# LayerNorm of a convolution module on one core: the variance of the first 256 tokens from the mean of seven channel blocks, corrected by the eighth

## The chip, the cores and the metric

The kernel runs on one core of one Trainium2 chip. The metric is the device time in microseconds (us) of one execution, as the median over runs. Five engines work at once, each through its own queue of instructions in order: TensorE (PE in the profile), VectorE (DVE), ScalarE (ACT), GpSimd (POOL) and the sync engine (SP), which only issues transfers. They wait for one another through semaphores. SBUF is the on-chip memory, PSUM the memory into which PE accumulates.

## The reference

Two layers with 512 tokens of 1024 channels. Layer 0 has a convolution module as its mixer, layer 1 an attention; each is followed by a squared-ReLU MLP. Only this part of layer 0 is touched:

```python
def layernorm(x, g, b):
    xf = x.astype(jnp.float32)
    mu = jnp.mean(xf, axis=-1, keepdims=True)
    var = jnp.mean(jnp.square(xf - mu), axis=-1, keepdims=True)
    y = (xf - mu) * lax.rsqrt(var + LN_EPS)
    return (y * g.astype(jnp.float32) + b.astype(jnp.float32)).astype(x.dtype)

def conformer_conv(h, pw1_w, pw1_b, dw_w, dw_b, ln_g, ln_b, pw2_w, pw2_b):
    a = h @ pw1_w + pw1_b
    u, gate = jnp.split(a, 2, axis=-1)
    u = u * jax.nn.sigmoid(gate)
    y = lax.conv_general_dilated(u, dw_w[:, None, :], ...) + dw_b   # 31 taps, causal, one filter per channel
    y = layernorm(y, ln_g, ln_b)
    y = jax.nn.silu(y)
    return y @ pw2_w + pw2_b
```

The mean and the variance are taken over the 1024 channels, for each token by itself.

## The kernel before, in words

Activations lie with channels on the 128 partitions: `y[:, k, :]` is channel block k (k = 0 to 7, `KB` = 8) for all 512 tokens. A sum over channels therefore needs PE: a matmul with a matrix of ones. Float32 matmuls are issued by PE as two passes each, so the profile counts two MATMUL rows for one in the code. `EARLY` is tokens 0 to 255, `LATE` tokens 256 to 511; the norm handles EARLY first, so that the second pointwise product (`second_conv`) can begin on it.

The order of work is written out by hand, engine by engine.

- **The last taps.** The taps of the depthwise convolution are shared by PE (`conv`, L1055 on), DVE (`tap`), ACT and POOL (`tap_sums`, L672). Block 7 is the last: DVE joins its partial sums (L2342), waits for POOL's sums (L2345), waits for PE's taps and writes `y[:, 7, :]` (L2348). In the meantime PE has begun the channel sum of blocks 0 to 6 into the PSUM bank STAT (L1079, L1080).
- **The mean.** PE adds block 7 to that sum (L1121). DVE then subtracts sum/D from each block (`conv_sub`, L2352): eight EARLY blocks, then three LATE ones.
- **The variance, EARLY.** ACT squares each EARLY block (L1707) into `m`. PE sums the squares over channels with eight calls of `token_columns` (L948), each two matmuls that move one column of ones. ACT takes the root (L1712), DVE the reciprocal (L2212), PE spreads it over the partitions (L955).
- **The norm loop, DVE.** For k = 0 to 8: `conv_norm` (L2362) multiplies `y` by the spread reciprocal in PSUM; one or no LATE `conv_sub`; `conv_rest` (L2368) makes the low part of the split of the result, `hlo = tmp - hhi`, after ACT's SiLU and copy (L1722, L1725); `late_add` (L2376) adds up LATE squares, which POOL makes (L803). So 5 LATE subtractions lie before the loop and 3 in it.
- **PE beside the loop.** `second_conv` multiplies each EARLY block by four weight units, 12 matmuls of 256 columns a block (L894 to L896), as soon as `hlo` of that block is there. After block 5 it waits for the seventh `late_add` (semaphore `c_add`), sums the LATE squares (L948), and after block 6 it spreads the LATE reciprocal (L955). The rest of the module, the MLP and layer 1 follow in series.
- **POOL's own queue** here: `tap_sums` of block 7, then four `conv_lo` (L677, 1024 elements per partition each, the low parts of the weights of the second pointwise product), then the eight LATE squares (L803).

`keep_warm` (L905) issues small matmuls with no use for their result. What matters of an operand is where it lies: `conv_sub` and `conv_norm` read one tensor of SBUF and one of PSUM; `conv_rest` and `late_add` read two tensors of SBUF.

```python
            for k in range(KB + 1):
                if k < KB:
                    conv_norm(0, k)
                if k < 3:
                    conv_sub(1, 5 + k)
                if k >= 1:
                    conv_rest(0, k - 1)
                if k >= 2:
                    late_add(k - 1)
```

Of the kernel before, what the change touches and what calls it, by code (L numbers as in the profile page):

```python
# [10 lines left out]
P = 128  # L11
# [197 lines left out]
def build(nc, x, g_mix_pre, g_mix_post, g_ffn_pre, g_ffn_post, conv_pw1_w, conv_pw1_b, conv_dw_w,  # L209
# [168 lines left out]
    form_hi, form_nth, form_lo, lo_nth = s["glu_s"], KB, s["c_ready"], 2 * KB  # L378
    h_made, made_nth = s["c_sub"], 2 * KB
    x_copy = nc.dram_tensor("x_copy", (P, KB * S), F32, kind="Internal").ap()  # L380
# [114 lines left out]
    with nc.Block() as block:  # L495
# [128 lines left out]
        def _(pool):  # L624
# [176 lines left out]
            for k in range(KB):  # L801
                pool.wait_ge(s["c_sub"], KB + k + 1)
                g.tensor_tensor(m[:, k, LATE], y[:, k, LATE], y[:, k, LATE], ALU.mult).then_inc(s["c_late"], 1)  # L803
# [74 lines left out]
        def _(pe):  # L878
# [180 lines left out]
            def conv(j, r, more=0):  # L1059
# [17 lines left out]
                if more:  # L1077
                    pe.wait_ge(s["y_sum"], y_sums(KB - 1) + 1)
                    pe.matmul(psum[:, STAT, :], ones[:, :], sumsq[:, :], start=True, stop=False)  # L1079
                    pe.matmul(psum[:, STAT, :], ones[:, :], y[:, KB - 2, :], start=False, stop=False)  # L1080
                    pe.wait_ge(s["diag"], KB - 1)
# [36 lines left out]

            keep_warm(WARM_TAPS)
            pe.wait_ge(s["y_done"], KB)  # L1120
            pe.matmul(psum[:, STAT, :], ones[:, :], y[:, KB - 1, :], start=False,  # L1121
                      stop=True).then_inc(s["mean"], 1)
            keep_warm(WARM_SUB, 0)
            for k in range(KB):
                pe.wait_ge(s["c_sq"], k + 1)
                mm = token_columns(OUTP, 0, m[:, k, :], (0, 1), k == 0, k == KB - 1)
            mm.then_inc(s["c_sum"], 1)
            keep_warm(WARM_ROOT, 0)
            pe.wait_ge(s["irms_done"], NTH[ST_VAR[0]])
# [14 lines left out]
            for kb in range(KB):  # L1144
                second_conv(0, (kb,), range(4))
                if kb == 5:
                    pe.wait_ge(s["c_add"], KB - 1)
# [327 lines left out]
        def _(act):  # L1475
# [229 lines left out]
            for k in range(KB):  # L1705
                act.wait_ge(s["c_sub"], k + 1)
                a.activation(m[:, k, EARLY], y[:, k, EARLY], ACT.Square).then_inc(s["c_sq"], 1)  # L1707

            def conv_root(h):
                tiles = (slice(0, 2), slice(2, 4))[h]  # L1710
                act.wait_ge(s["c_sum"], h + 1)
                a.activation(rms[:, tiles], psum[:, (OUTP, STAT)[h], tiles], ACT.Sqrt, scale=1.0 / D,  # L1712
                             bias=eps[:, 1:2]).then_inc(s["root"], 1)

# [457 lines left out]
        def _(dve):  # L2172
# [166 lines left out]
            for i in range(DVE_TAPS - MORE_TAPS):  # L2339
                tap(KB - 1, 1, i, DVE_TAPS - MORE_TAPS)  # L2340
            dve.wait_ge(s["tap"], DVE_TAPS * KB - MORE_TAPS)
            d.tensor_tensor(psum[:, 0, :], psum[:, 0, :], acc1[:, 1, :], ALU.add).then_inc(s["acc"], 1)  # L2342
            dve.wait_ge(s["acc"], KB)
            dve.wait_ge(s["y_sum"], y_sums(KB - 1) + (POOL_SUMS + 1))
            d.tensor_tensor(acc1[:, 1, :], psum[:, 0, :], y[:, KB - 1, :], ALU.add).then_inc(s["acc"], 1)  # L2345
            dve.wait_ge(s["acc"], KB + 1)
            dve.wait_ge(s["conv_done"], KB)
            d.tensor_tensor(y[:, KB - 1, :], psum[:, 5, :], acc1[:, 1, :], ALU.add).then_inc(s["y_done"], 1)  # L2348

            def conv_sub(h, k):  # L2350
                rows = (EARLY, LATE)[h]
                d.scalar_tensor_tensor(y[:, k, rows], psum[:, STAT, rows], -1.0 / D, y[:, k, rows], ALU.mult,  # L2352
                                       ALU.add).then_inc(s["c_sub"], 1)

            def conv_norm(h, k):
                rows = (EARLY, LATE)[h]
                if k == 0:
                    dve.wait_ge(s["bcast"], NTH[ST_VAR[h]])
                dve.wait_ge(s["c_sub"], KB * h + k + 1)
                if h:  # L2360
# [10 lines left out]
            def late_add(k):  # L2371

                dve.wait_ge(s["c_late"], k + 1)
                if k > 1:
                    dve.wait_ge(s["c_add"], k - 1)
                d.tensor_tensor(sumsq[:, LATE], m[:, 0, LATE] if k == 1 else sumsq[:, LATE], m[:, k, LATE],  # L2376
                                ALU.add).then_inc(s["c_add"], 1)

            dve.wait_ge(s["mean"], 1)
            for k in range(KB):  # L2380
                conv_sub(0, k)
            for k in range(3):
# [746 lines left out]
```

## Time and profile before

| what | value |
|---|---|
| median of 3 runs | 1138.76 us (1137.33 to 1139.12) |
| the profiled execution, its own time | 1139.56 us |
| its span, first to last instruction | 1137.8 us |
| mean granted TensorE clock in it | 0.996 of full |
| PE, DVE, ACT, POOL busy, share of the span | 98%, 82%, 67%, 26% |

The time axis of all rows is the span of the profiled execution. Its own time lies 1.76 us above the span and 0.80 us above the median. The norm of the convolution lies at about 150 to 186 us of that axis. A busy share is an average over the whole span; what limits a stage is read from the rows of that stage. In the timeline views a row is one or several alike instructions in order of time: start, length, engine, line of the kernel, operation, what it writes and reads, count, and in brackets how long the engine idled before it and who released it.

### The profile page before, as it was taken

The numbers are of one execution on the slowest core, as the hardware profiler recorded it, in microseconds if no ns is written. First come the engines' busy times: TensorE is split into PE (matmuls) and PEld (weight loads), VectorE is DVE, ScalarE is ACT, GpSimd is POOL, SyncE is SP. The second block draws the span as 40 slices with busy tenths as digits, with TensorE's granted clock in tenths as the row PEclk, the third lists the DMA queues.
The fourth block names the chain that finished last, engine by engine and source line by source line (L and its number), as shares of the span: only waits on it lengthen the run. The fifth ranks groups of instructions, "written<-read, shape, count | busy, mean of one in ns | idle before, by whom it ended". The sixth has DMA issues, their size and how long they took to land. (4 is left out here: it accounts for less than half of the span.)

```text
span 1137.8 us, 18248 instructions
## 1 busy us (share of the span) xinstructions
PE 1116.8 (98%) x6462; PEld 978.5 (86%) x6462; DVE 934.6 (82%) x1348; ACT 765.5 (67%) x1266; POOL 291.7 (26%) x269
## 2 busy tenths in 40 slices
PE   9999999999999999999999999999999999999997
PEld 7788888978898998998887888878888998998986
DVE  6899965679889689688798888894789889688788
ACT  6778868556685484675787777776566783674764
POOL 5688870221211020112421111100312020111014
PEclk9999989999999999999999999999999999999999
DMA  5322141275866676595222423232476776567673
GB/s 162 105 74 74 37 124 42 61 221 149 180 174 132 200 156 158 134 237 112 57 56 67 104 65 87 84 84 74 140 205 156 184 167 180 120 145 193 159 197 99
DMA packets 137268, 146.73 MB, mean 129 GB/s; under 512 B 5949, under 2 KB 108349, under 8 KB 136682
## 3 DMA queue, kind: packets, MB, share of 16 engines
q1 hardware_dynamic: 112300, 109.68, 30.7%
q0 software_dynamic: 24816, 35.92, 19.8%
q8 instruction: 45, 0.74, 0.3%
q14 instruction: 29, 0.24, 0.1%
q10 hardware_dynamic: 78, 0.16, 0.0%
HBM read 137.09 MB, written 6.29 MB: 126 GB/s over the span
## 5 line engine op out<-in xcount | busy, mean ns | idle before, releaser
L1525 ACT ACTIVATE whi<-mraw 128x1024 fp32r<-128x1024 f32 x212 | 221.4, 1055 | 150.3 <-PE psum L1219 92.0
L2190 DVE TENSOR_TENSOR wlo<-mraw,whi 128x1024 fp32r<-128x1024 f32 x212 | 256.7, 1222 | 71.5 <-ACT whi L1525 71.1
L1217 PE MATMUL psum<-whi,aop_hi 128*128 128x512 f32 x448 | 176.1, 393 | 1.0 <-ACT acc L1815 0.7
L1218 PE MATMUL psum<-wlo,aop_hi 128*128 128x512 f32 x448 | 174.5, 390 | 0.0
L1219 PE MATMUL psum<-whi,aop_lo 128*128 128x512 f32 x448 | 174.5, 389 | 0.0
L887 PE MATMUL psum<-hhi,whi 128*128 128x512 f32 x376 | 150.8, 401 | 0.8 <-DVE wlo L2179 0.5
L889 PE MATMUL psum<-hhi,wlo 128*128 128x512 f32 x376 | 147.0, 391 | 0.0
L888 PE MATMUL psum<-hlo,whi 128*128 128x512 f32 x376 | 146.8, 390 | 0.0
L1204 PE MATMUL psum<-xlo,whi 128*128 128x256 f32 x384 | 108.7, 283 | 0.0
L1205 PE MATMUL psum<-hhi,wlo 128*128 128x256 f32 x384 | 108.7, 283 | 0.0
L1203 PE MATMUL psum<-hhi,whi 128*128 128x256 f32 x384 | 108.6, 283 | 0.0
L1217 PEld LDWEIGHTS psum<-whi,aop_hi 128*128 128x128 f32 x448 | 84.1, 188 | 21.7 <-DVE acc L2653 2.5
L1219 PEld LDWEIGHTS psum<-whi,aop_lo 128*128 128x128 f32 x448 | 84.1, 188 | 17.8
L1218 PEld LDWEIGHTS psum<-wlo,aop_hi 128*128 128x128 f32 x448 | 84.2, 188 | 16.8
L889 PEld LDWEIGHTS psum<-hhi,wlo 128*128 128x128 f32 x376 | 70.6, 188 | 15.5
L887 PEld LDWEIGHTS psum<-hhi,whi 128*128 128x128 f32 x376 | 70.7, 188 | 14.7 <-issue 1.8
L888 PEld LDWEIGHTS psum<-hlo,whi 128*128 128x128 f32 x376 | 70.8, 188 | 12.9
L1203 PE MATMUL psum<-hlo,whi 128*128 128x256 f32 x288 | 81.6, 283 | 0.2 <-DVE pair L2594 0.2
L1205 PE MATMUL psum<-hlo,wlo 128*128 128x256 f32 x288 | 81.5, 283 | 0.0
L2269 DVE SCALAR_TENSOR_TENSOR psum<-upad,vec,psum 128x512 f32<-128x512 f32 x116 | 78.0, 749 | 3.4 <-ACT psum L1657 3.4
L761 POOL DMA_DIRECT2D mraw<-in_mlp_w_down x24 | 28.9, 1203 | 182.3 <-DVE wlo L2190 182.3
L1204 PEld LDWEIGHTS psum<-xlo,whi 128*128 128x128 f32 x384 | 73.7, 192 | 0.2
(314 smaller groups left out, 2834.8 us busy)
## 6 DMA issues: line engine op xcount, KB each, us to landing
mraw<-in_mlp_w_up SPq DMA_DIRECT2D x64, 512.0 KB, 7.0
mraw<-in_mlp_w_down SPq DMA_DIRECT2D x64, 512.0 KB, 5.5
mraw<-in_mlp_w_down POOLq DMA_DIRECT2D x40, 512.0 KB, 7.2
mraw<-in_mlp_w_up POOLq DMA_DIRECT2D x24, 512.0 KB, 7.1
wraw<-in_conv_pw_w SPq DMA_DIRECT2D x20, 512.0 KB, 4.5
wraw<-in_attn_w_in SPq DMA_DIRECT2D x16, 512.0 KB, 5.0
x_copy<-xT SPq DMA_DIRECT2D x2, 2048.0 KB, 7.4
xT<-x_copy SPq DMA_DIRECT2D x2, 2048.0 KB, 11.4
```

Of the source, the lines that this page charges most:

```text
L887: pe.matmul(o, whi[:, u, kb, :], xhi, start=start, stop=False)
L888: pe.matmul(o, whi[:, u, kb, :], xlo, start=False, stop=False)
L889: return pe.matmul(o, wlo[:, u, kb, :], xhi, start=False, stop=stop)
L1203: pe.matmul(o, wh[:, w], xh[:, k, :], start=first, stop=False, skip_group_check=True)
L1204: pe.matmul(o, wh[:, w], xl[:, k, :], start=False, stop=False, skip_group_check=True)
L1205: mm = pe.matmul(o, wl[:, w], xh[:, k, :], start=False, stop=k == 3, skip_group_check=True)
L1217: pe.matmul(o, ah, wh, start=kt == 0 and (not kept or c == 0), stop=False)
L1218: pe.matmul(o, ah, wl, start=False, stop=False)
L1219: return pe.matmul(o, al, wh, start=False, stop=kt == 3 and (not kept or c == CHUNKS - 1))
L1525: a.activation(split_unit(whi, e), raw_unit(l, c, e_), ACT.Copy).then_inc(s["m_hi"], 1)
L2190: d.tensor_tensor(split_unit(wlo, e), raw_unit(l, c, e_), split_unit(whi, e).bitcast(F32), ALU.subtract).then_inc(s["m_ready"], 1)
L2269: d.scalar_tensor_tensor(dst, upad[:, r, t:t + S], vcol(V_DW + t, j), src, ALU.mult, ALU.add).then_inc(s["tap"], 1)
```

## The change

For the EARLY tokens only, the variance is taken in another way. Blocks 0 to 6 are complete before block 7, so their sum S7 stands in PSUM while the last taps still run. DVE subtracts S7/(D-128) from blocks 0 to 6 (`first_sub`), and from the partial sum `acc1` of block 7, so that block 7 when finished has had the same number taken off. ACT squares these. What is left of the mean is the channel sum of block 7 alone over D, since the other seven now sum to zero; the sum of squares about the true mean is the sum of the squares less (sum of block 7)^2/D. DVE makes that correction on two columns (`tot`), and ACT's root reads it. The remaining mean is subtracted from EARLY by eight `conv_sub` that run beside the sums.

To sum fewer columns, DVE adds squares in pairs, blocks 0+1, 2+3, 4+5 (`early_add`, two SBUF tensors), so PE does five `token_columns` of squares and one of block 7 in place of eight. All eight LATE subtractions now lie in the norm loop. Two of the groups of `keep_warm` (2 and 3 matmuls) are gone, and the sum for the mean of LATE (with its own last step) comes after the column sums.

```diff
                     pe.matmul(psum[:, STAT, :], ones[:, :], sumsq[:, :], start=True, stop=False)
-                    pe.matmul(psum[:, STAT, :], ones[:, :], y[:, KB - 2, :], start=False, stop=False)
+                    pe.matmul(psum[:, STAT, :], ones[:, :], y[:, KB - 2, :], start=False,
+                              stop=True).then_inc(s["mean"], 1)
...
-            keep_warm(WARM_TAPS)
+            for k in (0, 2):
+                pe.wait_ge(s["c_add"], k // 2 + 1)
+                token_columns(OUTP, 0, m[:, k, :], (0, 1), k == 0, False)
             pe.wait_ge(s["y_done"], KB)
-            pe.matmul(psum[:, STAT, :], ones[:, :], y[:, KB - 1, :], start=False,
+            pe.matmul(psum[:, 1, LATE], ones[:, :], y[:, KB - 1, EARLY], start=True,
                       stop=True).then_inc(s["mean"], 1)
-            keep_warm(WARM_SUB, 0)
-            for k in range(KB):
+            token_columns(5, 0, y[:, KB - 1, :], (0, 1), True, True).then_inc(s["mean"], 1)
+            pe.wait_ge(s["c_add"], 3)
+            token_columns(OUTP, 0, m[:, 4, :], (0, 1), False, False)
+            for k in (KB - 2, KB - 1):
                 pe.wait_ge(s["c_sq"], k + 1)
-                mm = token_columns(OUTP, 0, m[:, k, :], (0, 1), k == 0, k == KB - 1)
+                mm = token_columns(OUTP, 0, m[:, k, :], (0, 1), False, k == KB - 1)
             mm.then_inc(s["c_sum"], 1)
+            pe.matmul(psum[:, STAT, LATE], ones[:, :], y[:, KB - 1, LATE], start=False, stop=True,
+                      skip_group_check=True).then_inc(s["mean"], 1)
             keep_warm(WARM_ROOT, 0)
...
+            def first_sub(t, sem):
+
+                d.scalar_tensor_tensor(t, psum[:, STAT, EARLY], -1.0 / (D - P), t, ALU.mult,
+                                       ALU.add).then_inc(sem, 1)
+
+            def early_add(k):
+
+                dve.wait_ge(s["c_sq"], k + 2)
+                d.tensor_tensor(m[:, k, EARLY], m[:, k, EARLY], m[:, k + 1, EARLY],
+                                ALU.add).then_inc(s["c_add"], 1)
...
+            dve.wait_ge(s["mean"], 1)
+            for k in range(KB - 1):
+                first_sub(y[:, k, EARLY], s["c_sub"])
             dve.wait_ge(s["acc"], KB)
             dve.wait_ge(s["y_sum"], y_sums(KB - 1) + (POOL_SUMS + 1))
             d.tensor_tensor(acc1[:, 1, :], psum[:, 0, :], y[:, KB - 1, :], ALU.add).then_inc(s["acc"], 1)
             dve.wait_ge(s["acc"], KB + 1)
+            first_sub(acc1[:, 1, EARLY], s["acc"])
+            early_add(0)
+            early_add(2)
+            dve.wait_ge(s["acc"], KB + 2)
             dve.wait_ge(s["conv_done"], KB)
             d.tensor_tensor(y[:, KB - 1, :], psum[:, 5, :], acc1[:, 1, :], ALU.add).then_inc(s["y_done"], 1)
...
-            dve.wait_ge(s["mean"], 1)
-            for k in range(KB):
+            early_add(4)
+            dve.wait_ge(s["mean"], 2)
+            conv_sub(0, 0)
+            conv_sub(0, 1)
+            dve.wait_ge(s["mean"], 3)
+            d.tensor_copy(tot[:, 0:2], psum[:, 5, 0:2]).then_inc(s["x_tot"], 1)
+            conv_sub(0, 2)
+            dve.wait_ge(s["x_tot"], 2)
+            d.scalar_tensor_tensor(tot[:, 2:4], tot[:, 0:2], -1.0 / D, psum[:, 5, 0:2], ALU.mult,
+                                   ALU.mult).then_inc(s["x_tot"], 1)
+            for k in range(3, 5):
                 conv_sub(0, k)
-            for k in range(3):
-                conv_sub(1, k)
+            dve.wait_ge(s["c_sum"], 1)
+            dve.wait_ge(s["x_tot"], 3)
+            d.tensor_tensor(tot[:, 2:4], psum[:, OUTP, 0:2], tot[:, 2:4], ALU.add).then_inc(s["x_tot"], 1)
+            conv_sub(0, 5)
+            conv_sub(0, 6)
             inverse(ST_VAR[0], slice(0, 2))
-            for k in range(3, 5):
-                conv_sub(1, k)
+            conv_sub(0, 7)
+            dve.wait_ge(s["mean"], 4)
             for k in range(KB + 1):
                 if k < KB:
                     conv_norm(0, k)
-                if k < 3:
-                    conv_sub(1, 5 + k)
+                if k < KB:
+                    conv_sub(1, k)
```

Semaphore counts elsewhere follow, and ACT's root of EARLY reads `tot` where it read PSUM. Three places show the order of instructions.

**DVE, from the last join of block 7 to the first subtractions.** Names: `acc_77` is `acc1`; 128x256 is one block of EARLY or LATE. Before:

```order
L2342 TENSOR_TENSOR psum<-psum,acc_77 128x512
L2345 TENSOR_TENSOR acc_77<-psum,y 128x512
L2348 TENSOR_TENSOR y<-psum,acc_77 128x512
L2352 SCALAR_TENSOR_TENSOR y<-psum,y 128x256 x11
L2212 RECIPROCAL irms<-rms 128x2
L2352 SCALAR_TENSOR_TENSOR y<-psum,y 128x256 x2
```

and in the changed kernel:

```order
L2365 TENSOR_TENSOR psum<-psum,acc_77 128x512
L2356 SCALAR_TENSOR_TENSOR y<-psum,y 128x256 x7
L2371 TENSOR_TENSOR acc_77<-psum,y 128x512
L2356 SCALAR_TENSOR_TENSOR acc_77<-psum,acc_77 128x256
L2362 TENSOR_TENSOR m<-m 128x256 x2
L2378 TENSOR_TENSOR y<-psum,acc_77 128x512
L2362 TENSOR_TENSOR m<-m 128x256
L2384 SCALAR_TENSOR_TENSOR y<-psum,y 128x256 x2
L2416 COPY tot<-psum 128x2
L2384 SCALAR_TENSOR_TENSOR y<-psum,y 128x256
L2419 SCALAR_TENSOR_TENSOR tot<-tot,psum 128x2
L2384 SCALAR_TENSOR_TENSOR y<-psum,y 128x256 x2
```

Seven subtractions now stand ahead of the wait for POOL's sums, and two of the pairwise additions (L2362) ahead of the instruction that finishes block 7 (L2378).

**DVE in the norm loop, k = 2 and 3.** Before:

```order
L2362 TENSOR_TENSOR y<-y,psum 128x256
L2352 SCALAR_TENSOR_TENSOR y<-psum,y 128x256
L2368 TENSOR_TENSOR hlo<-tmp,hhi 128x256
L2376 TENSOR_TENSOR sumsq<-m 128x256
L2362 TENSOR_TENSOR y<-y,psum 128x256
L2368 TENSOR_TENSOR hlo<-tmp,hhi 128x256
L2376 TENSOR_TENSOR sumsq<-sumsq,m 128x256
```

and in the changed kernel:

```order
L2394 TENSOR_TENSOR y<-y,psum 128x256
L2384 SCALAR_TENSOR_TENSOR y<-psum,y 128x256
L2400 TENSOR_TENSOR hlo<-tmp,hhi 128x256
L2408 TENSOR_TENSOR sumsq<-m 128x256
L2394 TENSOR_TENSOR y<-y,psum 128x256
L2384 SCALAR_TENSOR_TENSOR y<-psum,y 128x256
L2400 TENSOR_TENSOR hlo<-tmp,hhi 128x256
L2408 TENSOR_TENSOR sumsq<-sumsq,m 128x256
```

From k = 3 on each turn has a subtraction (L2384) that it did not have.

**PE between the last tap and the spread.** Before:

```order
L1073 MATMUL psum<-uhi,diaglo 128x512
L905 MATMUL psum<-ones 128x128 x2
L1121 MATMUL psum<-y,ones 128x512
L905 MATMUL psum<-ones 128x128 x3
L948 MATMUL psum<-ones,m 128x1 x16
L905 MATMUL psum<-ones 128x128
L955 MATMUL psum<-ident,irms 128x128 x2
```

and in the changed kernel:

```order
L1073 MATMUL psum<-uhi,diaglo 128x512
L948 MATMUL psum<-ones,m 128x1 x4
L1124 MATMUL psum<-y,ones 128x256
L948 MATMUL psum<-ones,y 128x1 x2
L948 MATMUL psum<-ones,m 128x1 x6
L1133 MATMUL psum<-y,ones 128x256
L905 MATMUL psum<-ones 128x128
L955 MATMUL psum<-ident,irms 128x128 x2
```

Four of the ten column sums of squares now stand ahead of block 7's own sum, six behind it.

## Rows read from the trace of the kernel before

**Rows 1.** The page, busy time of each engine over the span

```profile
PE 1116.8 (98%) x6462; PEld 978.5 (86%) x6462; DVE 934.6 (82%) x1348; ACT 765.5 (67%) x1266; POOL 291.7 (26%) x269
```

**Rows 2.** Timeline of PE, 151 to 175 us

```profile
151.44 0.61 PE L905 MATMUL psum<-ones 128*128 128x128 f32 x4
152.46 1.13 PE L1121 MATMUL psum<-y,ones 128*128 128x512 f32 x2 [0.41 <-DVE y L2348]
...
154.54 5.24 PE L948 MATMUL psum<-ones,m 128*128 128x1 f32 x32 [0.29 <-ACT m L1707]
...
160.34 1.22 PE L955 MATMUL psum<-ident,irms 128*128 128x128 f32 x4
...
164.13 0.36 PE L894 MATMUL psum<-hhi,whi 128*128 128x256 f32 x1
...
172.83 0.50 PE L948 MATMUL psum<-ones,sumsq 128*128 128x1 f32 x4
...
174.71 0.60 PE L955 MATMUL psum<-ident,irms 128*128 128x128 f32 x4
```

**Rows 3.** Timeline of DVE, 149 to 162 us

```profile
149.85 0.69 DVE L2345 TENSOR_TENSOR acc<-psum,y 128x512 f32<-128x512 f32 x1 [2.99 <-POOL y L672]
151.71 0.69 DVE L2348 TENSOR_TENSOR y<-psum,acc 128x512 f32<-128x512 f32 x1 [1.17 <-PE psum L1073]
153.62 3.73 DVE L2352 SCALAR_TENSOR_TENSOR y<-psum,y 128x256 f32<-128x256 f32 x11 [1.22 <-PE psum L1121]
160.11 0.17 DVE L2212 RECIPROCAL irms<-rms 128x2 f32<-128x2 f32 x1 [2.76 <-ACT rms L1712]
...
161.59 0.42 DVE L2362 TENSOR_TENSOR y<-y,psum 128x256 f32<-128x256 f32 x1 [0.66 <-PE psum L955]
```

**Rows 4.** Timeline of ACT, 154 to 160 us

```profile
154.08 2.73 ACT L1707 ACTIVATE m<-y 128x256 f32<-128x256 f32 x8 [4.23 <-DVE y L2352]
159.82 0.26 ACT L1712 ACTIVATE rms<-psum,eps 128x2 f32<-128x2 f32 x1 [3.01 <-PE psum L948]
```

**Rows 5.** Timeline of DVE, turn k = 2 of the norm loop and its end

```profile
163.91 0.41 DVE L2362 TENSOR_TENSOR y<-y,psum 128x256 f32<-128x256 f32 x1
164.24 0.41 DVE L2352 SCALAR_TENSOR_TENSOR y<-psum,y 128x256 f32<-128x256 f32 x1
164.57 0.41 DVE L2368 TENSOR_TENSOR hlo<-tmp,hhi 128x256 fp32r<-128x256 f32 x1
164.90 0.83 DVE L2376 TENSOR_TENSOR sumsq<-m 128x256 f32<-128x256 f32 x1
165.66 0.41 DVE L2362 TENSOR_TENSOR y<-y,psum 128x256 f32<-128x256 f32 x1
...
171.95 0.42 DVE L2376 TENSOR_TENSOR sumsq<-sumsq,m 128x256 f32<-128x256 f32 x1
```

**Rows 6.** Timeline of POOL, 149 to 166 us

```profile
149.71 9.34 POOL L677 TENSOR_TENSOR wlo<-wraw,whi 128x1024 fp32r<-128x1024 f32 x4
158.99 2.91 POOL L803 TENSOR_TENSOR m<-y 128x256 f32<-128x256 f32 x5
...
164.72 0.73 POOL L803 TENSOR_TENSOR m<-y 128x256 f32<-128x256 f32 x1 [1.02 <-DVE y L2352]
```

**Rows 7.** Timelines of DVE, then POOL, 61 to 65 us

```profile
61.73 1.75 DVE L2294 SCALAR_TENSOR_TENSOR upad<-tmp,vec 128x512 f32<-128x512 f32 x1
...
61.65 1.29 POOL L686 TENSOR_TENSOR y<-y,acc 128x512 f32<-128x512 f32 x1
63.02 1.62 POOL L690 TENSOR_TENSOR sumsq<-sumsq,y 128x512 f32<-128x512 f32 x1
```

**Rows 8.** Windows: us, busy per engine (instructions), PEclk, DMA share, GB/s

```profile
151.60:156.50 4.90, 4.20 (x31) 3.33 (x29) 3.57 (x10) 2.42 (x8) 4.90 (x3) 1.00 0.18 51
156.50:163.30 6.80, 6.80 (x32) 6.59 (x33) 3.25 (x11) 3.28 (x7) 6.22 (x9) 0.50 0.78 269
```

**Rows 9.** Timeline of PE asked for 157 to 157.9 us only

```profile
156.66 1.42 PE L948 MATMUL psum<-ones,m 128*128 128x1 f32 x6
```

More of the change, by code:

```diff
@@ L378, in build @@
     form_hi, form_nth, form_lo, lo_nth = s["glu_s"], KB, s["c_ready"], 2 * KB
-    h_made, made_nth = s["c_sub"], 2 * KB
+    h_made, made_nth = s["c_sub"], 3 * KB - 1
     x_copy = nc.dram_tensor("x_copy", (P, KB * S), F32, kind="Internal").ap()
@@ L801, in _ @@
             for k in range(KB):
-                pool.wait_ge(s["c_sub"], KB + k + 1)
+                pool.wait_ge(s["c_sub"], 2 * KB + k)
                 g.tensor_tensor(m[:, k, LATE], y[:, k, LATE], y[:, k, LATE], ALU.mult).then_inc(s["c_late"], 1)
@@ L1146, in _ @@
                 if kb == 5:
-                    pe.wait_ge(s["c_add"], KB - 1)
+                    pe.wait_ge(s["c_add"], KB + 2)
                     token_columns(STAT, 0, sumsq, (2, 3), True, True).then_inc(s["c_sum"], 1)
@@ L1705, in _ @@
             for k in range(KB):
-                act.wait_ge(s["c_sub"], k + 1)
+                if k < KB - 1:
+                    act.wait_ge(s["c_sub"], k + 1)
+                else:
+                    act.wait_ge(s["y_done"], KB)
                 a.activation(m[:, k, EARLY], y[:, k, EARLY], ACT.Square).then_inc(s["c_sq"], 1)
@@ L1710, in conv_root @@
                 tiles = (slice(0, 2), slice(2, 4))[h]
-                act.wait_ge(s["c_sum"], h + 1)
-                a.activation(rms[:, tiles], psum[:, (OUTP, STAT)[h], tiles], ACT.Sqrt, scale=1.0 / D,
-                             bias=eps[:, 1:2]).then_inc(s["root"], 1)
+                if h == 0:
+                    act.wait_ge(s["x_tot"], 4)
+                else:
+                    act.wait_ge(s["c_sum"], 2)
+                a.activation(rms[:, tiles], psum[:, STAT, tiles] if h else tot[:, 2:4], ACT.Sqrt,
+                             scale=1.0 / D, bias=eps[:, 1:2]).then_inc(s["root"], 1)
             def conv_silu(h):
@@ L2351, in conv_sub @@
                 rows = (EARLY, LATE)[h]
-                d.scalar_tensor_tensor(y[:, k, rows], psum[:, STAT, rows], -1.0 / D, y[:, k, rows], ALU.mult,
-                                       ALU.add).then_inc(s["c_sub"], 1)
+                if h == 0:
+                    dve.wait_ge(s["c_sq"], k + 1)
+                d.scalar_tensor_tensor(y[:, k, rows], psum[:, STAT if h else 1, LATE], -1.0 / D, y[:, k, rows],
+                                       ALU.mult, ALU.add).then_inc(s["c_sub"], 1)
             def conv_norm(h, k):
@@ L2358, in conv_norm @@
                     dve.wait_ge(s["bcast"], NTH[ST_VAR[h]])
-                dve.wait_ge(s["c_sub"], KB * h + k + 1)
+                dve.wait_ge(s["c_sub"], KB * (h + 1) + k)
                 if h:
@@ L2374, in late_add @@
                 if k > 1:
-                    dve.wait_ge(s["c_add"], k - 1)
+                    dve.wait_ge(s["c_add"], k + 2)
                 d.tensor_tensor(sumsq[:, LATE], m[:, 0, LATE] if k == 1 else sumsq[:, LATE], m[:, k, LATE],
                                 ALU.add).then_inc(s["c_add"], 1)
-            dve.wait_ge(s["mean"], 1)
-            for k in range(KB):
-                conv_sub(0, k)
-            for k in range(3):
-                conv_sub(1, k)
+            early_add(4)
[9 more added lines that the diff above has]
+            for k in range(3, 5):
+                conv_sub(0, k)
+            dve.wait_ge(s["c_sum"], 1)
[3 more added lines that the diff above has]
+            conv_sub(0, 6)
             inverse(ST_VAR[0], slice(0, 2))
-            for k in range(3, 5):
-                conv_sub(1, k)
+            conv_sub(0, 7)
+            dve.wait_ge(s["mean"], 4)
             for k in range(KB + 1):
```

## The prediction, made before the changed kernel was run

> **What bounds the kernel now.** I first read the page's busy times: PE is busy for 98% of the span [rows 1], so nearly all delays of PE reach the end one for one, and the question is where PE waits or idles in useless work around the norm. The timeline of PE shows it [rows 2]. The taps end at about 151.6 us; from there to 164.13, when the second product begins (L894), PE does only small work: the mean (L1121), 32 passes of column sums in 5.24 us (L948), the spread (L955) and keep_warm. That is 12.5 us of serial chain, which I followed through the timelines of DVE and ACT [rows 3, 4]: block 7 written at 151.71, mean until 153.59, first subtraction at 153.62, first square at 154.08, last square over at 156.81, column sums over at 159.78, root at 159.82, reciprocal at 160.11, first norm at 161.59. Call this last moment T. PE starts at T + 2.54. Then PE itself is the limit: from 164.13 to 172.83 it does six blocks, 1.45 us each [rows 2]. At 172.83 it asks for the last late_add, which ended at 172.37 [rows 5], so nothing waits there, but only by 0.46 us.
>
> **What shares a path.** The rows that decide for me are about DVE and POOL. L2294 reads two SBUF tensors. It started at 61.73, while POOL's L686 ran to 62.94, and ended at 63.48, 0.54 us after POOL; POOL's next instruction took 1.62 us in place of 1.29 [rows 7]. L2376 (two SBUF tensors, 256 elements) took 0.83 us in place of 0.42 when POOL's L803 ran from 164.72 to 165.45, and ended 0.28 us after it [rows 5, 6]. But eleven L2352 (one SBUF, one PSUM operand) ran 0.34 us apart while POOL was in L677 without a pause [rows 3, 6]. So in this trace a DVE instruction with two SBUF inputs and a POOL instruction take turns, whole instruction by whole instruction, and others pass freely.
>
> **The change part by part.**
>
> *Seven first_sub on blocks 0 to 6* (one SBUF operand): 7 x 0.34 = 2.4 us, in the 2.99 us in which DVE idled until POOL's sums came at 149.85 [rows 3]. Nothing. Were this gap gone they would cost 2.4. The eighth, on acc1, takes 0.34 of the 1.17 us idle before L2348 [rows 3]: nothing; it ends at 151.0. ACT's squares of blocks 0 to 6 then come during that time, and four of them are done by 151.3.
>
> *early_add(0) and (2), ahead of block 7.* They add two SBUF tensors while POOL is in its four L677, 9.34 / 4 = 2.34 us each, from 149.71 on [rows 6]. early_add(0) is issued at 150.9 and must wait until the first L677 ends at 152.05; it ends at 152.33 (the 0.28 above). POOL's second L677 has been waiting and goes next, as L690 did [rows 7], until 154.67; early_add(2) ends at 154.95. Behind it on DVE stands the instruction that finishes block 7: it needs neither, but starts at 154.9 where it started at 151.71, **3.2 us late**. early_add(4) waits for the third L677 and ends at 157.6. No row shows a hold by an instruction of 1024 elements. The bounds are no hold at all (0) and the whole 2.34 us; I take the whole, since at 256 and at 512 elements POOL held for all of its row.
>
> The Trainium skill, SBUF — State Buffer, section SBUF: two separate sides, says the same of any length: DVE and GpSimd share one port pair as an exclusive lock for a whole instruction, also against DVE instructions with two SBUF inputs. By that rule the sum is the one I make; by the shortest hold the rows allow for it would be about 4.9 us less.
>
> *Mean and column sums on PE.* Block 7's own sums take less than 1 us and are over by 156.9. PE then waits for early_add(4): of the squares, blocks 4+5, 6 and 7 remain, 12 passes. At half clock 6 passes take 1.42 us, 0.21 start to start with the last one's 0.35 [rows 9]; at full clock 4 take 0.50 [rows 2], about 0.1 each. The clock was at 0.50 from 156.5 to 163.3 [rows 8], so I take 0.21: 2.5 us, over at 160.2 (full clock: 158.9).
>
> *Correction, root, reciprocal.* The small DVE instructions cost as L2212, 0.17 us. The correction goes 160.2 to 160.4, the root 0.26 [rows 4]; on DVE two subtractions (0.68) stand ahead of the reciprocal, which starts at 161.0. Before, 1.48 us lay from its start to the first norm [rows 3]: T = 162.5, **+0.9 us**. At full clock five subtractions and two small instructions behind 157.5 end at 159.4, the reciprocal follows at 160.2 and the spread is 0.6 shorter (0.60 against 1.22 [rows 2]): T = 161.05, -0.5. PE's late mean (L1133) and the fewer keep_warm lie beside this; the five keep_warm saved lay in waits and give nothing. ACT's table for SiLU loads beside the reciprocal and spread as before.
>
> *The norm loop.* Five more LATE subtractions stand in it; before, they lay in the shadow of the column sums, so nothing is won there. The turn k = 2 of before has just the four instructions that turns 2 to 7 now have: norm 163.91, subtraction 164.24, rest 164.57, late_add 164.90 with 0.83 us, next norm 165.66 [rows 5]. That is 1.75 us: the subtraction's end releases POOL's square (L803), which takes its turn after the rest and holds the late_add [rows 6]. Each turn repeats this. So norm k starts at T + 2.32 + 1.75 (k - 2), norm 7 at T + 11.07, and the eighth turn's rest and late_add end at T + 13.57. Before, PE asked for this at T + 11.24. **+2.4 us.** The low bound is 4 x 0.335 = 1.34 us a turn, no hold: last late_add at T + 11.5, +0.3. With 1.75 against PE's 1.45 a block, DVE also becomes the limit of the first blocks, but this is all inside the 2.4. What follows (column sums of LATE, root, spread, second half) keeps its order and shifts.
>
> **The sum**: +0.9 + 2.4 = +3.3 us. On the profiled execution's 1139.56 that is 1142.9; that execution lay 0.80 over the median, so on the median **1142.0**. About 0.2% (2.3 us) is what a measurement of this kernel can tell from no change; the forecast is 0.29%. Its own range: 1140.0 to 1143.3, from T at -0.5 or +0.9 and turns somewhat shorter than 1.75.
>
> **The rivals.**
>
> *B, DVE wins twice.* If early_add(2) gets in right behind early_add(0), before POOL's second L677, block 7 is finished from 152.6 on, early_add(4) ends at 155.3, the correction falls at 157.2, the reciprocal at 158.0 and T at 159.5, -2.1. With the loop's +2.4: 1139.1. For it: the two additions are 0.3 us apart; against it: L690 took its turn at once behind one DVE instruction [rows 7], and so did L803 between rest and late_add [rows 5, 6].
>
> *C, L677 does not hold DVE, but the squares do.* Block 7 at 151.7, five subtractions and the correction until 155.3, reciprocal 156.1, T = 157.6, -4.0; loop +2.4: 1137.2. For it: no row shows L677 holding anything.
>
> *D, faster: neither hold matters.* The place is DVE's L2362 at 151 us and its late_add in the loop; the price is -4.0 at T and +0.3 in the loop, 1135.1. It decides when L2362 takes 0.42 us beside a running L677 and turns take under 1.45, PE's own pace. Then the shorter chain counts in full. Against it stand both pairs of rows named above.
>
> *E, much slower: both two-SBUF instructions of a turn are held.* If POOL's square comes so that the rest waits as well, 0.4 more in each of six turns is 2.4 on top, and 1144.5 comes out. For it: POOL is in no step with DVE by design; against it, one square per turn can hold once.
>
> The clock is not a rival of its own: were the second product to begin at half clock, 2.9 us a block, the 2.4 us that PE would wait for the last late_add absorb 3.3 us and more of it.
>
> **How the numbers follow.** The forecast (A) has 0.60, B 0.15, C 0.08, D 0.08, E 0.09. Slower by over 0.2% means above 1141.0: four fifths of A and E, 0.57. Faster by over 0.2% means below 1136.5: D and a tail of C, 0.10. The rest, 0.33, is within. The range, 1137.0 to 1144.0, holds A, B and most of C, and leaves out D and most of E.
>
> **What would show it.** In the changed kernel's timeline: first_sub x7 inside the gap, ending before 149.3; L2362 x2 at 151 us with about 1.4 and 2.6 us for 0.42; L2378 at 154.9; root at about 160.5 and first norm near 162.5; turns of 1.75 us with L2408 at 0.83; and PE idle 1.5 us or more after the sixth EARLY block, released by L2408. If L2378 starts before 153, B, C or D holds. If PE doesn't idle after the sixth block, the term of the loop is wrong. If the first norm comes before 160 and the time is still above 1141, the loss lies somewhere that I don't see.

## The result, and the profile after

| | before | changed |
|---|---|---|
| median of 6 runs each | 1138.86 us (1137.29 to 1139.23) | 1144.22 us (1143.05 to 1146.54) |
| ratio to before, 95% interval | | 1.0054 [1.0043, 1.0064] |
| the profiled execution, its own time | 1139.56 us | 1143.05 us |
| its span; mean granted TensorE clock | 1137.8 us; 0.996 | 1141.1 us; 0.992 |

The change costs 5.4 us by the medians, where 3.3 were forecast: slower, as foreseen, and 0.2 us above the upper end of the range. One run of early_psum below and one run of the kernel before on each of two chips took 1353 to 3891 us; all medians and intervals here leave these three out. The two traces agree on the start of POOL's first L677 within 0.1 us (149.71 before, 149.79 now), so the rows below can be compared as they stand.

DVE in the changed kernel, timeline from the early subtractions to the first norm, against [rows 3]:

```profile
146.85 2.40 DVE L2356 SCALAR_TENSOR_TENSOR y<-psum,y 128x256 f32<-128x256 f32 x7
149.93 0.69 DVE L2371 TENSOR_TENSOR acc<-psum,y 128x512 f32<-128x512 f32 x1 [0.69 <-POOL y L672]
150.66 0.42 DVE L2356 SCALAR_TENSOR_TENSOR acc<-psum,acc 128x256 f32<-128x256 f32 x1
151.00 3.95 DVE L2362 TENSOR_TENSOR m<-m 128x256 f32<-128x256 f32 x2
154.88 0.68 DVE L2378 TENSOR_TENSOR y<-psum,acc 128x512 f32<-128x512 f32 x1
155.48 1.97 DVE L2362 TENSOR_TENSOR m<-m 128x256 f32<-128x256 f32 x1
...
160.33 0.16 DVE L2425 TENSOR_TENSOR tot<-psum,tot 128x2 f32<-128x2 f32 x1 [1.09 <-PE psum L948]
160.41 0.74 DVE L2384 SCALAR_TENSOR_TENSOR y<-psum,y 128x256 f32<-128x256 f32 x2
161.07 0.15 DVE L2225 RECIPROCAL irms<-rms 128x2 f32<-128x2 f32 x1
...
162.73 0.42 DVE L2394 TENSOR_TENSOR y<-y,psum 128x256 f32<-128x256 f32 x1 [1.18 <-issue]
```

The seven early subtractions end at 149.25, inside the gap. The two `early_add` ahead of block 7 take 3.95 us in place of 0.75, the third 1.97, and the instruction that finishes block 7 starts at 154.88. The first norm, T in the prediction, is at 162.73 against 161.59: +1.14.

POOL, timeline of the same stretch and of the first loop turns, against [rows 6]:

```profile
149.79 9.87 POOL L677 TENSOR_TENSOR wlo<-wraw,whi 128x1024 fp32r<-128x1024 f32 x4
163.56 1.27 POOL L803 TENSOR_TENSOR m<-y 128x256 f32<-128x256 f32 x2 [3.90 <-DVE y L2384]
165.87 0.73 POOL L803 TENSOR_TENSOR m<-y 128x256 f32<-128x256 f32 x1 [1.03 <-DVE y L2384]
```

The four L677 took 9.34 us before and 9.87 now: the DVE instructions came between them.

DVE, timeline of loop turns k = 3 and 8, against [rows 5]:

```profile
166.80 0.41 DVE L2394 TENSOR_TENSOR y<-y,psum 128x256 f32<-128x256 f32 x1
167.13 0.41 DVE L2384 SCALAR_TENSOR_TENSOR y<-psum,y 128x256 f32<-128x256 f32 x1
167.46 0.41 DVE L2400 TENSOR_TENSOR hlo<-tmp,hhi 128x256 fp32r<-128x256 f32 x1
167.79 0.83 DVE L2408 TENSOR_TENSOR sumsq<-sumsq,m 128x256 f32<-128x256 f32 x1
168.55 0.41 DVE L2394 TENSOR_TENSOR y<-y,psum 128x256 f32<-128x256 f32 x1
...
175.55 0.41 DVE L2400 TENSOR_TENSOR hlo<-tmp,hhi 128x256 fp32r<-128x256 f32 x1
175.89 0.41 DVE L2408 TENSOR_TENSOR sumsq<-sumsq,m 128x256 f32<-128x256 f32 x1
```

A turn takes 1.75 us, with `late_add` (L2408) at 0.83, in all six turns.

PE, timeline, the small work of the norm, the start of the second product (L894) and the wait after its sixth block, against [rows 2]:

```profile
152.53 0.61 PE L948 MATMUL psum<-ones,m 128*128 128x1 f32 x4 [0.85 <-DVE m L2362]
155.01 1.01 PE L948 MATMUL psum<-ones,m 128*128 128x1 f32 x4 [1.87 <-DVE m L2362]
155.89 1.20 PE L1124 MATMUL psum<-y,ones 128*128 128x256 f32 x2
156.88 0.85 PE L948 MATMUL psum<-ones,y 128*128 128x1 f32 x4
157.59 2.70 PE L948 MATMUL psum<-ones,m 128*128 128x1 f32 x12
...
165.27 0.36 PE L894 MATMUL psum<-hhi,whi 128*128 128x256 f32 x1
...
176.35 0.61 PE L948 MATMUL psum<-ones,sumsq 128*128 128x1 f32 x4 [1.47 <-DVE sumsq L2408]
...
178.67 1.05 PE L955 MATMUL psum<-ident,irms 128*128 128x128 f32 x4
```

PE stood idle 1.47 us for the last `late_add`, and the column sums of LATE begin 3.52 us later than before (176.35 against 172.83). The spread behind them took 1.05 us where it took 0.60. The granted clock (PEclk, third number from the end) in windows around the norm, against [rows 8], says why:

```profile
157.00:160.00 3.00, 3.00 (x17) 3.00 (x15) 2.24 (x8) 0.00 (x0) 2.66 (x2) 0.50 0.64 221
...
166.00:175.00 9.00, 8.76 (x68) 8.09 (x67) 9.00 (x22) 5.31 (x12) 3.87 (x6) 1.00 0.95 239
175.00:178.00 3.00, 1.65 (x13) 1.65 (x14) 1.47 (x4) 2.77 (x5) 0.35 (x1) 0.98 0.01 3
178.00:181.00 3.00, 3.00 (x16) 3.00 (x15) 0.75 (x2) 1.51 (x4) 0.00 (x0) 0.50 0.00 0
181.00:184.00 3.00, 3.00 (x25) 2.92 (x24) 2.27 (x6) 2.90 (x7) 0.00 (x0) 0.95 0.00 0
```

Behind the wait there is a second stretch at half clock (1.2 in place of 2.4 GHz), from about 177.9 to 181.3 us by windows of 1 us; the kernel before has only the first one. So the norm's loss has three parts, and a fourth lies behind it. From the start of the LATE column sums to ACT's first write of the second product's result (a fixed piece of work) it takes 14.01 us here (176.35 to 190.36) and 13.12 before (172.83 to 185.95). ACT's timeline, that first write before and in the changed kernel:

```profile
185.95 0.69 ACT L1742 ACTIVATE m<-psum,vec 128x512 f32<-128x512 f32 x1 [0.99 <-PE psum L896]
190.36 0.69 ACT L1755 ACTIVATE m<-psum,vec 128x512 f32<-128x512 f32 x1 [0.98 <-PE psum L896]
```

| part | read at | forecast | measured |
|---|---|---|---|
| T, the first norm | 162.73 - 161.59 | +0.9 | +1.14 |
| the loop, up to the LATE column sums | 3.52 - 1.14 | +2.4 | +2.38 |
| second stretch at half clock | 14.01 - 13.12 | 0 | +0.89 |
| the norm, sum | 190.36 - 185.95 | +3.3 | +4.41 |
| behind it, by the medians | 5.36 - 4.41 | 0 | +0.95 |

### The profile page after: what moved, and what is told of

Read it like the earlier page. It is cut to its first block and busy times, and to the rows that moved or that the text cites. A ratio compares the mean times of both kernels' runs of the same rounds, so it can differ in the third digit from the quotient of the medians.

```text
span 1141.1 us, 18232 instructions
## 1 busy us (share of the span) xinstructions
PE 1116.9 (98%) x6446; PEld 978.5 (86%) x6446; DVE 944.7 (83%) x1362; ACT 765.3 (67%) x1266; POOL 293.5 (26%) x269
## 5 line engine op out<-in xcount | busy, mean ns | idle before, releaser
L887 PEld LDWEIGHTS psum<-hhi,whi 128*128 128x128 f32 x376 | 70.7, 188 | 15.3 <-issue 2.4
L1210 PEld LDWEIGHTS psum<-hhi,whi 128*128 128x128 f32 x384 | 73.7, 192 | 0.2
```

Of the source, the lines that this page charges most:

```text
L887: pe.matmul(o, whi[:, u, kb, :], xhi, start=start, stop=False)
L1210: pe.matmul(o, wh[:, w], xh[:, k, :], start=first, stop=False, skip_group_check=True)
```

## The experiments

**Theory.** POOL's L677 holds the `early_add`s and so block 7; POOL's squares (L803) hold `late_add`, one per turn; the wait that comes of it on PE costs clock as well. **Rivals.** The early part costs by its longer chain, whoever holds what; the loop is slow by its fifth to eighth subtraction, not by a hold; the second half-clock stretch is chance. Twelve more kernels ran. "Median against before" is against runs of the kernel before on the same chip (1138.20 to 1138.86 us); "ratio" goes with the same runs; "norm" is the shift of ACT's first write of the second product's result (185.95 in the first profile of before), less the shift of the start of POOL's first L677 (149.71 there, within 0.31 us of it in all).

| kernel | median, us | ratio [95%] | median against before | norm |
|---|---|---|---|---|
| changed | 1144.22 | 1.0054 [1.0043, 1.0064] | +5.4 | +4.3 |
| control | 1145.24 | 1.0062 [1.0050, 1.0075] | +7.0 | +4.2 |
| early_psum | 1138.98 | 1.0009 [1.0000, 1.0018] | +0.8 | -1.6 |
| late_psum | 1141.69 | 1.0031 [1.0019, 1.0043] | +3.5 | +1.3 |
| warm_stall | 1142.33 | 1.0038 [1.0024, 1.0051] | +4.1 | +3.5 |
| base | 1138.27 | 0.9997 [0.9988, 1.0006] | -0.1 | -0.2 |
| odd_psum | 1139.25 | 1.0008 [0.9998, 1.0017] | +0.9 | -1.6 |
| gate | 1142.27 | 1.0037 [1.0023, 1.0051] | +3.9 | +2.0 |
| odd_gate | 1137.95 | 0.9998 [0.9989, 1.0007] | -0.4 | -3.4 |
| delay2 | 1140.39 | 1.0016 [1.0003, 1.0029] | +1.8 | +2.1 |
| delay4 | 1142.36 | 1.0037 [1.0023, 1.0051] | +3.7 | +3.1 |
| odd_gate_last | 1137.24 | 0.9992 [0.9981, 1.0002] | -1.4 | -3.7 |
| warm_all | 1142.03 | 1.0036 [1.0020, 1.0052] | +3.4 | +2.0 |

**control**: the changed kernel again, no edit.

> The changed kernel itself, once more, beside the others on the same chip. Both theories: 1144.2 us median, 5.3 over before. The profile of the first run had span +3.3 us but a shift of 4.3 us at the end of the norm; if the place of the clock's drop varies between executions, this profile shows a half-clock stretch after the sixth EARLY block of another length, and the shift at the end of the module (ACT's first L1755 at 190.36 in the first profile, L1742 at 185.95 before) between 3.3 and 5.5.

1145.24 us. The norm is as in the first profile: PE waits 1.49 us, the second stretch at half clock lasts from about 178.2 to 181.6 us, and the norm is at +4.2. The median says +7.0, though: what the medians add to the norm of one profile is not stable between two sets of runs of one kernel.

**early_psum**: the `early_add`s with one operand in PSUM.

```diff
-                d.tensor_tensor(m[:, k, EARLY], m[:, k, EARLY], m[:, k + 1, EARLY],
-                                ALU.add).then_inc(s["c_add"], 1)
+                d.scalar_tensor_tensor(m[:, k, EARLY], psum[:, STAT, EARLY], 0.0, m[:, k, EARLY],
+                                       ALU.mult, ALU.add).then_inc(s["c_add"], 1)
```

> The three early_add are replaced by an instruction of the same output, size, place and waits that reads one SBUF tensor and one PSUM tensor (times zero), so the odd squares are left out of the sum of squares of EARLY. Theory (taking turns with POOL's L677 holds them): they take 0.42 us each, block 7 is finished from 151.8 in place of 154.9, the first norm comes at about 157.7 (162.7 in the changed kernel), and all later work shifts by 5.0: 1139.2 us. Rival (they are late for their wait on ACT's squares or cost by themselves): block 7 stays near 154.9 and the time near 1144.2.

DVE's timeline in early_psum:

```profile
151.24 0.75 DVE L2362 SCALAR_TENSOR_TENSOR m<-psum,m 128x256 f32<-128x256 f32 x2
152.01 0.69 DVE L2378 TENSOR_TENSOR y<-psum,acc 128x512 f32<-128x512 f32 x1
...
157.78 0.42 DVE L2394 TENSOR_TENSOR y<-y,psum 128x256 f32<-128x256 f32 x1 [1.18 <-issue]
```

Same place, same element count, POOL in L677 as before, and 0.75 us in place of 3.95. The first norm is at 157.78, 4.95 us earlier than in the changed kernel and 3.8 earlier than before (4.1 when the axes are set alike). Rivals C and D of the prediction gave -4.0 for just this. So the hold is worth 5 us at T, with what it does to the clock (the twelve passes behind it took 1.69 us here, 2.70 in the changed kernel), and the change without it would win 4 there.

**late_psum**: `late_add` with one operand in PSUM.

```diff
-                d.tensor_tensor(sumsq[:, LATE], m[:, 0, LATE] if k == 1 else sumsq[:, LATE], m[:, k, LATE],
-                                ALU.add).then_inc(s["c_add"], 1)
+                d.scalar_tensor_tensor(sumsq[:, LATE], psum[:, STAT, LATE], 0.0,
+                                       m[:, 0, LATE] if k == 1 else sumsq[:, LATE], ALU.mult, ALU.add).then_inc(s["c_add"], 1)
```

> late_add in the norm loop reads PSUM (times zero) and one SBUF tensor in place of two SBUF tensors; all LATE squares but block 0 are left out of the sum. Theory (the square on POOL holds late_add once a turn, and the wait that this gives PE also lets its clock fall): turns of 1.35 to 1.45 us in place of 1.75, PE does not idle after the sixth EARLY block, no half-clock stretch there: 2.4 + 1.1 less, 1140.7 us. Rival 1 (the clock's drop is not due to this idle): 2.4 less, 1141.8. Rival 2 (five more instructions in the loop are the cost, whatever they read): turns stay over 1.6 us and the time over 1143.

DVE's timeline, one turn, and PE's:

```profile
167.34 0.41 DVE L2408 SCALAR_TENSOR_TENSOR sumsq<-psum,sumsq 128x256 f32<-128x256 f32 x1
167.68 0.40 DVE L2394 TENSOR_TENSOR y<-y,psum 128x256 f32<-128x256 f32 x1
168.01 0.41 DVE L2384 SCALAR_TENSOR_TENSOR y<-psum,y 128x256 f32<-128x256 f32 x1
168.34 0.40 DVE L2400 TENSOR_TENSOR hlo<-tmp,hhi 128x256 fp32r<-128x256 f32 x1
168.67 0.41 DVE L2408 SCALAR_TENSOR_TENSOR sumsq<-psum,sumsq 128x256 f32<-128x256 f32 x1
```

```profile
174.23 0.50 PE L948 MATMUL psum<-ones,sumsq 128*128 128x1 f32 x4
```

With all four instructions still in the turn, it takes 1.33 us, which was the prediction's low bound (1.34). PE no longer waits, the LATE column sums begin 2.12 us earlier, and there is no second stretch at half clock. From T (162.70) to the column sums it is 11.53 us, 0.3 more than before in place of 2.4, as that bound had it. The loss in the loop is the hold, not the added subtractions. In all the norm ends 3.0 us earlier (187.34 against 190.36), the median 2.5. By its median (1141.69) this run alone would speak for rival 1, that the clock is untouched (1141.8); the trace shows the stretch gone, so the figure doesn't decide this.

**warm_stall**: seven `keep_warm` where PE would wait for the last `late_add`, so that it is busy there.

```diff
+                    keep_warm(7)
                     pe.wait_ge(s["c_add"], KB + 2)
```

> Seven small matmuls of 128 columns without use (14 passes, 1.5 us at full clock) stand ahead of PE's wait for the last late_add, in the 1.47 us in which it idled. Theory (this idle is what lets the granted clock fall from 177.9 to 181.3): no half-clock stretch there, 1.1 us less: 1143.1. Rival (the drop comes from something else, or the 0.9 us that PE waits before it count as well): the stretch stays and the time stays at 1144.2, or rises by up to 0.3 where the matmuls last longer than the wait.

PE's timeline:

```profile
174.45 1.72 PE L905 MATMUL psum<-ones 128*128 128x128 f32 x14
176.09 0.61 PE L948 MATMUL psum<-ones,sumsq 128*128 128x1 f32 x4
178.07 0.60 PE L955 MATMUL psum<-ident,irms 128*128 128x128 f32 x4
```

The column sums begin when they did (176.09), but the clock stays at 1.00 and the piece of work behind them takes 13.23 us (176.09 to 189.32) against 14.01 and, in control, 13.87. So a second stretch costs 0.6 to 0.8 us. The other 0.1 of the 0.89 is not the clock: 13.21 to 13.23 us is also what all five other profiles have in which the column sums do not follow the sixth block at once and no second stretch comes (early_psum, odd_psum, gate, odd_gate, odd_gate_last), and 13.10 to 13.13 is what those have in which they do (before, base, late_psum, delay2, delay4). The median fell by 2.9 us against control, more than this explains.

That filling the wait is what kept the clock up is likely but not shown. The stretch came in the two profiles of the changed kernel and in neither of the two with the wait filled (this one and warm_all), but it also stayed away in early_psum and odd_psum, with a wait as long; and in this profile the first half-clock stretch lay elsewhere too (about 156.0 to 162.8 us, in place of 154.0 to 164.1). The rival "chance" is not out.

**base**: the kernel before again.

> The kernel before, submitted as an experiment. Nothing changes: ratio 1.000 with an interval of about 0.1%. It is here for a second profile: in the first one, PE's waits between 195 and 540 us and between 800 and 1141 us add up to less or more than in the variants by up to 1.2 us each. If those waits (L1217 on ACT's L1815, L1217's operands on DVE's L2190) vary here as they do there, the shifts after the norm are chance of one execution; if they stay at 0.4 and 0.3, the variants have a cost of their own downstream.

1138.27 against 1138.35: this comparison adds nothing of its own. Its profile has a span 1.3 us shorter than the first one of before, 1.0 of it behind the norm, so one profile's span is no measure of a single us.

**odd_psum**: a real version of early_psum: ACT writes the squares of blocks 1, 3 and 5 into free PSUM banks, so that each `early_add` reads one tensor of each kind.

```diff
-                a.activation(m[:, k, EARLY], y[:, k, EARLY], ACT.Square).then_inc(s["c_sq"], 1)
+                to = psum[:, 2 + k // 2, EARLY] if k in (1, 3, 5) else m[:, k, EARLY]
+                a.activation(to, y[:, k, EARLY], ACT.Square).then_inc(s["c_sq"], 1)
...
-                d.tensor_tensor(m[:, k, EARLY], m[:, k, EARLY], m[:, k + 1, EARLY],
+                d.tensor_tensor(m[:, k, EARLY], m[:, k, EARLY], psum[:, 2 + k // 2, EARLY],
```

> Nothing left out: ACT writes the squares of EARLY blocks 1, 3 and 5 to three free PSUM banks, so each early_add reads one SBUF tensor and one PSUM tensor. Theory (only the second SBUF operand makes early_add wait for POOL): early_add takes 0.42 us, block 7 is finished by 151.8, the reciprocal starts 9.0 us after the first first_sub (14.2 in the changed kernel), and the median is that of early_psum, 1139.3. Rival (early_psum was faster since it left something else undone): reciprocal later by over 1 us and a median over 1141.

DVE's timeline, with the whole computation in place:

```profile
150.65 0.74 DVE L2363 TENSOR_TENSOR m<-m,psum 128x256 f32<-128x256 f32 x2
151.42 0.69 DVE L2379 TENSOR_TENSOR y<-psum,acc 128x512 f32<-128x512 f32 x1
...
157.43 0.42 DVE L2395 TENSOR_TENSOR y<-y,psum 128x256 f32<-128x256 f32 x1 [1.19 <-issue]
```

T is 3.9 us earlier than before (axes set alike: 3.9 = 161.59 - 157.43 - 0.27), the loop loses 2.2 again (170.88 - 157.43 against 11.24), and the norm is 1.6 us shorter in all; yet the median is 0.9 us above that of before.

**gate**: from block 2 on, POOL's LATE square waits until DVE's `late_add` of the turn is over, in place of starting behind the subtraction.

```diff
             for k in range(KB):
                 pool.wait_ge(s["c_sub"], 2 * KB + k)
+                if k >= 2:
+                    pool.wait_ge(s["c_add"], k + 2)
```

> The changed kernel with one more wait: POOL makes LATE square k (k from 2) only when late_add k-1 has ended, so that the square runs beside norm and subtraction, which read one SBUF tensor. Theory (it is the order of the turns at the port, not the work, that makes a turn 1.75 us): turns of 1.35 to 1.45 us, PE without a wait after the sixth EARLY block, no half-clock stretch there; 3.5 us under the changed kernel as late_psum was, 1141.2. Rival (the square then holds the rest instead of the late_add): turns stay at 1.7 or more, time 1144.5.

Timelines of DVE, then POOL, of one turn and of the last:

```profile
167.09 0.41 DVE L2410 TENSOR_TENSOR sumsq<-sumsq,m 128x256 f32<-128x256 f32 x1
...
168.47 0.41 DVE L2410 TENSOR_TENSOR sumsq<-sumsq,m 128x256 f32<-128x256 f32 x1
...
174.01 0.42 DVE L2410 TENSOR_TENSOR sumsq<-sumsq,m 128x256 f32<-128x256 f32 x1 [0.50 <-POOL m L805]
```

```profile
167.65 0.61 POOL L805 TENSOR_TENSOR m<-y 128x256 f32<-128x256 f32 x1 [0.76 <-DVE sumsq L2410]
```

The same instructions with the same operands: only the moment of POOL's square is another, and the turn is 1.38 us. The last `late_add` now waits 0.50 us for its square, so PE begins the column sums at 174.49, and its wait is 0.69 us, where none was expected. The norm gains 2.3 us against the changed kernel, the median 2.0 (1142.27, where 1141.2 was expected and 1144.5 by the rival).

**odd_gate** and **odd_gate_last**: both edits together; in the second one the last square is not held back (`if 2 <= k < KB - 1`).

> Both mends together, nothing left out. Theory: the two costs are apart from each other and add up. The end of the norm lies 3.9 us before that of the kernel before (1.6 from early_psum's profile and 2.4 from the loop), 1134.7 us; if the variants have a cost of up to 2 us downstream, 1136.7. Rival (the kernel before is bound elsewhere, so an earlier norm gives nothing): 1138.5.

> odd_gate with the added wait on squares 2 to 6 alone: the last square has no late_add beside it in its turn, yet its wait made PE idle 1.0 us after the sixth EARLY block. Theory: last late_add 0.5 to 0.7 us earlier, PE's wait 0.4 or less, 0.6 us under odd_gate: 1137.4 by median. Rival (no change by median, since a wait after the norm takes it): 1137.95.

The columns of LATE begin 3.3 and 3.6 us earlier than in before (PE's timeline, odd_gate_last):

```profile
169.24 0.61 PE L950 MATMUL psum<-ones,sumsq 128*128 128x1 f32 x4 [0.65 <-DVE sumsq L2411]
```

In the medians of 11 runs 0.4 and 1.4 us of this are left. Both beat the changed kernel by about 6 and 7 us; neither beats the kernel before by more than the measurement can tell (intervals up to 1.0007 and 1.0002). odd_gate missed both figures of its theory (1134.7, and 1136.7 with a cost downstream): 1137.95 is nearer to the rival's 1138.5. Still, an earlier norm does not give nothing: against gate, on the same chip, odd_gate's norm is 5.4 us earlier and its median 4.3 lower.

odd_gate_last came near its figure (1137.4), but PE waits 0.65 us, not 0.4 or less. Without the added wait, POOL's last square collides with the `late_add` of the turn before the last, which is held once more (DVE's timeline):

```profile
167.69 0.83 DVE L2411 TENSOR_TENSOR sumsq<-sumsq,m 128x256 f32<-128x256 f32 x1
```

**delay2**, **delay4**: the kernel before with the norm made longer by useless matmuls ahead of the second product, and nothing else.

```diff
-            keep_warm(WARM_NORM, 0)
+            keep_warm(18, 0)        # delay4: 28
```

> The kernel before with 18 in place of 8 keep_warm ahead of the second product: 20 more passes of 128 columns, about 0.11 us each at full clock, so the end of the norm moves by 2.2 us and nothing else changes. Theory (what follows the norm shifts one for one, and the rest of the changed kernel's loss is in the norm itself, where the clock falls in another way from run to run): 2.2 more, 1140.6. Rival (the part after the norm answers to a shift with waits of its own, as the waits of L1217 let one suspect): 3 us or more, or under 1.2.

> The same with 28 keep_warm: 40 more passes, 4.4 us. Theory: 1142.8. Rival: 1143.8 or more, by 1 us of added waits downstream, which would be the part of the changed kernel's 5.4 to 5.9 us that the 4.3 us at the end of the norm don't explain.

Norm +2.1 and +3.1, medians +1.8 and +3.7. A plain delay passes to the end about one for one, and brings no loss of its own. delay4 also shows how much hangs on where the first half-clock stretch falls. PE's timeline, 32 passes that took 5.24 us in [rows 2]:

```profile
154.41 3.73 PE L948 MATMUL psum<-ones,m 128*128 128x1 f32 x32 [0.30 <-ACT m L1707]
```

Here the clock fell at about 158.8, behind them; that is why the norm shifted by only 3.1 us.

**warm_all**: `keep_warm(7)` as in warm_stall, and PE kept busy in its two early waits as well.

```diff
+            keep_warm(4)
             for k in (0, 2):
+                if k:
+                    keep_warm(8, 0)
                 pe.wait_ge(s["c_add"], k // 2 + 1)
```

> warm_stall with two more fills, 8 and 16 passes of small matmuls in PE's waits of 0.85 and 1.87 us for the first two early_add. Theory (PE's idle there lets the clock fall before the twelve column sums): full clock until 157 or later, these sums in 1.5 in place of 2.7 us, the reciprocal up to 0.8 us earlier, as DVE's own subtractions bound it next; 1141.5 to 1142.0. Rival (the clock falls at 155 to 156.5 all the same, as in the kernel before): 1142.3.

PE's timeline, the 12 passes that took 2.70 us in the changed kernel:

```profile
157.13 1.50 PE L948 MATMUL psum<-ones,m 128*128 128x1 f32 x12 [0.85 <-DVE m L2366]
```

The clock stays at 1.00 until 160.0 us. With the axes set alike, the reciprocal (159.52) starts 1.2 us earlier than in the changed kernel, more than the 0.8 expected, and T (160.78) lies 1.6 us earlier. There is no second stretch, and the norm stands at +2.0; DVE's holds are still in it.

**What stays open.** In the table, the ten kernels with the change or a variant of it lie above their own norm's shift by 0.6 to 3.0 us in the median, 2.0 on average; the three without it (base, delay2, delay4) by 0.1 on average. So the change costs something more than the norms of the profiles show. Three parts can be told apart:

- A run's own time lies above its span by 1.93 to 1.96 us on average in each of the ten, and by 1.72 to 1.76 in every set of runs without the change. That is 0.2 us, steady, and outside all rows.
- In the profiled executions the rest of the span, from ACT's first write on, is 952.0 us on average in the ten (950.7 to 952.9) and 951.3 in before, base, delay2 and delay4 (950.8 to 951.9): 0.8 us, of the size of the scatter. Part of it can be PE's wait on ACT in the first MLP: 0.23 to 0.38 us in the four without the change, 1.14 to 1.45 in control, early_psum, odd_psum and odd_gate_last, but 0.53 or less in the other six, 0.17 in the changed kernel's first profile. In the second MLP, waits of up to 0.7 us come and go.
- The last 0.9 us (2.0 less 0.1, 0.2 and 0.8) lies between the profiled executions and the medians: the profiled ones of the ten are on average 0.5 us faster than their kernel's median. It may well lie in the norm itself, in executions of which there is no profile, since the half-clock stretches differ from profile to profile.

One profile per kernel can't settle the last two, and no run here does.

## Why the prediction was right in its steps, and short in its size

- **Seven `first_sub` for nothing**: right. 2.40 us, over at 149.25, before POOL's sums come.
- **`early_add` held by L677, block 7 3.2 us late**: right to 0.1 us (154.88 for 154.9), and shown by early_psum and odd_psum. The prediction took the whole 2.34 us with no row of a hold of that length, and the trace bears it out. By the Trainium skill, SBUF — State Buffer, section SBUF: two separate sides, the shared port pair is an exclusive lock for a whole instruction; the trace agrees at this length too (3.95 us for two additions). B (two turns in a row for DVE), C and D (no hold) are out.
- **T + 0.9**: +1.14 (+1.06 with the axes set alike; two profiles of the kernel before differ by 0.3 us in T themselves). Twelve passes took 2.70 us for the 2.5 forecast, and the correction came at 160.33 for 160.2. That the sums would run at half clock was taken from [rows 8] and was right.
- **Loop +2.4**: +2.38; turns of 1.75 us, one hold each, PE idle 1.47 us behind its sixth block where "1.5 us or more" was to be seen. late_psum and gate show that it is the hold. E (two holds a turn) is out.
- **The step that failed** is the one that priced the clock: "The clock is not a rival of its own: were the second product to begin at half clock, 2.9 us a block, the 2.4 us that PE would wait for the last late_add absorb 3.3 us and more of it." It looked only at the clock ahead of the wait, and took the wait itself for a cushion. In the changed kernel and in control the clock fell behind the wait, over the spread and a part of the next blocks, where nothing absorbs it: 0.89 us in place of 0, of which the stretch itself is 0.6 to 0.8 by warm_stall's profile. What decides whether it comes stays open: early_psum and odd_psum, with a wait as long, had none.
- **"What follows (column sums of LATE, root, spread, second half) keeps its order and shifts"** holds, to the end of the kernel, for a plain delay (delay2, delay4), not for this change: 0.95 us more in the first runs, 2.9 in control (7.04 - 4.16). 0.2 of it is the own time outside the span; the rest is measured and not explained. Of the 2.06 us that the forecast fell short, 0.89 is the clock, 0.95 this, 0.2 T. Without either of the two larger ones 1144.22 would be 1143.3, inside the range.

## What to carry to other kernels

When VectorE work with two SBUF inputs is put into a time in which GpSimd runs long instructions, price it at GpSimd's instruction, and look at what stands behind it in the queue: here 0.75 us of additions ahead of the last block cost 5 us. Two remedies were shown: put one operand into PSUM, or let GpSimd's instruction wait for the VectorE instruction with which it would collide. A wait of TensorE that a longer chain brings can be worth more than its length, since the clock can fall behind it (0.6 to 0.8 us here, in two profiles of four); and a win of 3 us in one stage is not yet a win in the time of the kernel.

## What the runs showed of the hardware

- DVE and POOL took turns instruction by instruction at 1024 elements too (3.95 us for two additions of 0.42), also where DVE had a second one ready at once: POOL's queued instruction went first each time.
- A wait of like length on PE, behind like work, brought half clock in two of four profiles: changed (1.47 us) and control (1.49) yes, early_psum (1.49) and odd_psum (1.46) no. With waits of 0.65 to 1.00 us (gate, odd_gate, odd_gate_last) it never did.
- Small matmuls of one column, 32 passes of the same work: 5.24, 4.95 and 5.33 us (before, base, delay2) and 3.73 where the clock fell later (delay4). Where the fall comes relative to the work is worth up to 1.6 us in this norm.
